# A two-layer encoder on one core: the MLP's down projections as seven block products in place of eight

## The reference, cut to what matters

```python
for i in range(2):
    h = h + mixer_i(rms_norm(h, norm_mix[i]))          # layer 0: conv + attention, layer 1: RWKV-7
    h = h + cross_attention(rms_norm(h, norm_xattn[i]), rms_norm(mem, norm_mem[i]), ...)
    h = h + squared_relu_mlp(rms_norm(h, norm_ffn[i]), ffn_w_up[i], ffn_w_down[i])
return rms_norm(h, norm_final)

def squared_relu_mlp(h, w_up, w_down):                 # (512, 1024), (1024, 4096), (4096, 1024)
    return jnp.square(jax.nn.relu(h @ w_up)) @ w_down
```

## Time and profile before

| | |
|---|---|
| device time, median of 3 | 1913.2 us (1911.54 to 1913.42) |
| span of the profiled execution, first to last instruction | 1909.6 us |
| TensorE busy | 97% of the span |
| VectorE, ScalarE, GpSimd busy | 55%, 39%, 9% |
| memory traffic | 189 MB, mean 99 GB/s |

### The profile page before, as it was taken

The page is one execution under the profiler, slowest core; times in us unless marked ns, Lnnn a source line. Parts: engine busy times, 40 slices in busy tenths (PEclk is TensorE's granted clock), DMA queues, the critical chain, the costliest instruction groups (busy, mean ns, idle before and its releaser), DMA issues.

```text
span 1909.6 us, 38661 instructions
## 1 busy us (share of the span) xinstructions
PE 1857.5 (97%) x17053; PEld 1527.4 (80%) x17053; DVE 1052.6 (55%) x1405; ACT 747.2 (39%) x999; POOL 168.8 (9%) x135
## 2 busy tenths in 40 slices
PE   6999999999999999999999999999999999999997
PEld 5898658778888888785779999998787788888886
DVE  4897655444432442447659888887654344324422
ACT  4434664334422332223544434343643343213322
POOL 1000002000000000210013111111020010000000
PEclk9999999999999999999999999999999999999999
DMA  6226223213332232453442112112362123332221
GB/s 215 89 71 233 78 100 133 66 45 93 106 111 88 89 111 88 137 159 127 154 147 62 51 50 53 49 31 70 126 217 70 44 89 102 97 110 89 88 88 44
DMA packets 165503, 189.41 MB, mean 99 GB/s; under 512 B 11801, under 2 KB 152646, under 8 KB 163674
## 3 DMA queue, kind: packets, MB, share of 16 engines
q1 hardware_dynamic: 162016, 174.44, 28.8%
q0 software_dynamic: 3088, 12.45, 1.7%
q10 hardware_dynamic: 234, 0.06, 0.0%
HBM read 161.22 MB, written 21.51 MB: 96 GB/s over the span
## 4 chain that ended last, share of the span: by engine, by line
PE 51%; DVE 3%; ACT 2%; issue 1%; DMA 1%; ACTq 0%; DVEq 0%
PE ps L357 11%; PE ps L358 10%; PE ps L359 10%; PE ps L2372 7%; PE ps L2338 2%; PE ps L2385 1%; PE ps L2326 1%; PE ps L1706 1%; PE ps L2349 1%; PE ps L1313 1%; PE ps L1746 1%; PE ps L2468 1%; ACT weights_split L326 1%; PE ps L2305 1%; PE ps L1294 1%
## 5 line engine op out<-in xcount | busy, mean ns | idle before, releaser
L344 DVE TENSOR_TENSOR weights_split<-w,weights_split 128x2048 fp32r<-128x2048 f32 x117 | 268.1, 2291 | 243.1 <-ACT weights_split L326 238.2
L326 ACT ACTIVATE weights_split<-w 128x2048 fp32r<-128x2048 f32 x118 | 225.9, 1914 | 285.7 <-PE ps L359 265.9
L357 PE MATMUL ps<-x_hn_hi,weights_split 128*128 128x512 f32 x640 | 252.7, 395 | 0.0
L359 PE MATMUL ps<-x_hn_hi,weights_split 128*128 128x512 f32 x640 | 249.2, 389 | 0.0
L358 PE MATMUL ps<-x_hn_lo,weights_split 128*128 128x512 f32 x640 | 249.0, 389 | 0.0
L357 PE MATMUL ps<-f_hidden_hi,weights_split 128*128 128x512 f32 x512 | 199.3, 389 | 0.0
L359 PE MATMUL ps<-f_hidden_hi,weights_split 128*128 128x512 f32 x512 | 199.2, 389 | 0.0
L358 PE MATMUL ps<-f_hidden_lo,weights_split 128*128 128x512 f32 x512 | 199.2, 389 | 0.0
L1565 DVE SCALAR_TENSOR_TENSOR f_relu<-ps,x_squares 128x512 f32<-128x512 f32 x64 | 44.1, 692 | 191.1 <-PE ps L359 172.5
L358 PEld LDWEIGHTS ps<-x_hn_lo,weights_split 128*128 128x128 f32 x640 | 120.2, 188 | 26.3 <-issue 1.4
L357 PEld LDWEIGHTS ps<-x_hn_hi,weights_split 128*128 128x128 f32 x640 | 120.1, 188 | 26.2 <-issue 1.4
(11 more groups left out here) (365 smaller groups left out, 3464.0 us busy)
## 6 DMA issues: line engine op xcount, KB each, us to landing
w<-in_ffn_w_up_dram SPq DMA_DIRECT2D x32, 1024.0 KB, 5.4
w<-in_ffn_w_down_dram SPq DMA_DIRECT2D x32, 1024.0 KB, 5.0
w<-in_xattn_w_kv_dram SPq DMA_DIRECT2D x15, 1024.0 KB, 5.4
w<-in_ab_w_in_dram SPq DMA_DIRECT2D x10, 1024.0 KB, 5.1
w<-in_xattn_w_q_dram SPq DMA_DIRECT2D x8, 1024.0 KB, 5.0
w<-in_xattn_w_o_dram SPq DMA_DIRECT2D x8, 1024.0 KB, 4.9
w<-in_ab_w_out_dram SPq DMA_DIRECT2D x4, 1024.0 KB, 5.5
w<-in_rwkv_w_r_dram SPq DMA_DIRECT2D x4, 1024.0 KB, 5.9
```

The costliest lines, as they stand in the source:

```text
L326: act.activation(hi, raw, ACT.Copy).then_inc(k.w_hi_ready, 1)
L344: eng.tensor_tensor(lo, raw, hi.bitcast(F32), ALU.subtract).then_inc(k.w_lo_ready, 1)
L357: pe.matmul(out, lhs[0], rhs[0], start=start, stop=False)
L359: return pe.matmul(out, lhs[1], rhs[0], start=False, stop=stop)
```

## The change

The MLP runs in four quarters of 1024 hidden channels. In each, the product of the hidden values (512 x 1024) with the down weights (1024 x 1024) is cut into halves of all three dimensions, and the eight products of blocks become seven products of sums of blocks, with four differences of weight blocks and four sums of hidden blocks. A product (P1 to P7) has the hidden values as the stationary operand and weights as the moving one, so results are token rows: two tiles of 128 tokens x 512 channels, 24 matmuls of 512 columns with 128 rows in the array. There are 7 units of weights in a quarter to be split, each used for 24 matmuls; before, a quarter's worth was 4 slots of 48. VectorE makes the four differences of raw weights (`combine`, 128x2048), GpSimd the sums of hidden blocks (three of 128x256) and their remainders (128x768) for each of the 4 hidden blocks of a quarter. Finished products are taken out of PSUM by VectorE into two sums of token rows (`take`, 14 of 128x512 a quarter). Five products share banks 4 to 7 one behind the other (`FORMER`), so P4, say, may begin when P7 is taken.

At the end of layer 0 the token rows are transposed back in 32 transposes and added to h, then squared and added up, all of it behind the last product. In layer 1, h is transposed to token rows during the first quarter (32 transposes, copied by ScalarE), and the output's norm is computed on token rows, rows 2 and 3 (tokens 256 to 511) ahead of the last product's end. A fourth raw buffer (`f_weights`) lies over the squares' buffers; its first load waits for the norm's factor.

```diff
@@ plan_weights, in layer_tail (one quarter: 4 slots of up weights, then 4 blocks of down weights) @@
-            for half in range(0, FF, FF // 2):
-                cols(f"up{l}", i["ffn_w_up"][l], half, half + FF // 2)
-                for c in range(0, D, SLOT):
-                    for r in range(half, half + FF // 2, D):
-                        cols(f"down{l}", i["ffn_w_down"][l], c, c + SLOT, r)
+            for r in range(0, FF, D):
+                cols(f"up{l}", i["ffn_w_up"][l], r, r + D)
+                rows = i["ffn_w_down"][l][r:r + D, :].rearrange("(j k p) c -> k p j c", k=2, p=P)
+                for b, n in ((0, 1), (1, 1), (0, 0), (1, 0)):
+                    self.slots.append((f"down{l}", [(None, None, rows[b, :, :, n * D // 2:(n + 1) * D // 2])]))
...
+                    x12, x22, x11, x21 = range(s - 3, s + 1)
+                    n = len(self.units)
+                    self.units += [(x11, 0), (x21, 0), (x11, sums + 1), (x11, sums + 3), (x22, 0), (x12, sums + 2),
+                                   (x21, sums + 4)]
@@ Split: the difference of two raw weight blocks, written over one of them @@
+    def combine(self, dve, i, a, b):
...
+        dve.tensor_tensor(flat(s), flat(sa), flat(sb), ALU.subtract).then_inc(k.w_sums, 1)
@@ stage_layer @@
+    PRODUCTS = (("P1", 0, 4, 0, 0, 0), ("P2", 3, None, 1, 0, 0), ("P5", 4, 6, 2, 1, 1), ("P6", 5, 4, 3, 0, 1),
+                ("P3", 6, 6, 4, 0, 1), ("P7", 1, 4, 5, 1, 1), ("P4", 2, 4, 6, 1, 0))
+    FORMER = {"P6": ("P1", 0), "P3": ("P5", 0), "P7": ("P6", 0), "P4": ("P7", 0), "P1": ("P4", 1), "P5": ("P3", 1)}
...
@@ TensorE @@
+            def down(q):
+                for x, (name, part, bank, u, half, right) in enumerate(PRODUCTS):
+                    ws.wait(pe, WF + NS * q + 4 + u)
...
+                        mm = mm3(pe, outs[m], [h[:, j, part, m * P:(m + 1) * P] for h in hid],
+                                 ws.wide_pair(WF + NS * q + 4 + u, j), j == 0 and name in ("P1", "P2", "P5"), j == 3,
+                                 bank is not None)
...
+                    if last and q == 0:
+                        for c in (2 * a, 2 * a + 1):
+                            k.take(pe, turned[c])
+                            for t in range(4):
+                                m = pe.transpose(k.bank(turned[c])[:, t * P:(t + 1) * P],
+                                                 k.h[:, c, t * P:(t + 1) * P], k.ident)
...
+            if not last:
+                for n, c in enumerate(TURN):
+                    k.take(pe, turned[n])
...
+                squares[2].sum(pe)
@@ ScalarE @@
+            for q in range(4):
                 for a in range(4):
...
+                    for m in range(3):
+                        b = PARTS[m]
+                        if m == 1:
+                            ws.round(act, WF + NS * q + a + 2)
+                        if m < 2:
+                            k.wait_freed(act, up[q][2 * a + m])
+                            r = tm[:, 3 * m:3 * m + 2, :]
+                            act.activation(r, r, ACT.Square).then_inc(s_hsq, 1)
...
+                        else:
+                            act.wait_ge(s_hsum, 2 * y + 1)
+                        act.activation(hid[0][:, a, b.start - 1:b.stop - 1, :], tm[:, b, :], ACT.Copy).then_inc(s_hhi, 1)
...
+                for x in range(7):
+                    ws.round(act, WF + NS * q + 4 + x + 2)
@@ VectorE @@
+            for q in range(4):
...
                 for a in range(4):
...
+                    relu(q, a, 0)
...
+                    dve.tensor_tensor(tm[:, 2, :], tm[:, 1, :], tm[:, 0, :], ALU.subtract).then_inc(s_hd, 1)
+                    remainder(q, a, 0)
+                    relu(q, a, 1)
+                    ws.rest(dve, W + a + 2)
+                    remainder(q, a, 1)
+                    if a == 2:
+                        ws.combine(dve, U + 2, U + 5, U)
+                    elif a == 3:
+                        ws.combine(dve, U + 5, U + 4, U + 5)
+                for x in range(7):
...
+                    late = x in (0, 1, 3)
+                    if not late:
+                        take(q, x)
+                    ws.rest(dve, U + x + 2)
+                    if x == 0:
+                        ws.combine(dve, U + 3, U + 4, U + 2)
+                    elif x == 2:
+                        ws.combine(dve, U + 6, U + 1, U + 3)
+                    if late:
+                        take(q, x)
+                    if last and q == 3 and x == 4:
...
+                        for t in (2, 3):
+                            root(t, t + 3)
+                            scaled(t, 0)
+                            scaled(t, 1)
...
+                for n, c in enumerate(TURN):
+                    k.wait_full(dve, turned[n])
+                    dve.tensor_tensor(k.h[:, c, :], k.bank(turned[n]), k.h[:, c, :], ALU.add) \
@@ GpSimd @@
+            for y in range(y0, y0 + 16):
+                pool.wait_ge(s_hsq, 2 * y + 2)
...
+                k.pool.link(pool, pool.tensor_tensor(tm[:, 5, :], tm[:, 0, :], tm[:, 3, :], ALU.add))
+                k.pool.link(pool, pool.tensor_tensor(tm[:, 6, :], tm[:, 5, :], tm[:, 1, :], ALU.subtract))
+                pool.tensor_tensor(tm[:, 7, :], tm[:, 4, :], tm[:, 6, :], ALU.subtract).then_inc(s_hsum, 1)
+                pool.wait_ge(s_hhi, 3 * y + 3)
+                pool.tensor_tensor(hid[1][:, y % 4, 4:7, :], tm[:, 5:8, :], hid[0][:, y % 4, 4:7, :].bitcast(F32),
+                                   ALU.subtract).then_inc(s_hsum, 1)
```

More of the change, by code:

```diff
@@ L262, in split_room, with slot_plan @@
         self.w_lo = [room[:, 3], room[:, 1]]
-    def slot_plan(self, jobs, split=True):
+    def slot_plan(self, jobs, split=True, slots=None):
         s0 = self.at
@@ L284, in w_wait @@
     def w_wait(self, pe, s):
-        need = sum(16 * len(self.slots[t][1]) for t in range(s % NW, s + 1, NW))
-        pe.wait_ge(self.w_in[s % NW], need)
+        b = self.buffers[s]
+        need = sum(16 * len(self.slots[t][1]) for t in range(s + 1) if self.buffers[t] == b)
+        pe.wait_ge(self.w_in[b], need)
 class Split:
@@ L296, in __init__ @@
         self.k, self.base = k, k.splits
-        assert k.to_split[self.base] == s0, "slots are split in order"
+        assert k.units[self.base][0] == s0, "slots are split in order"
         k.splits += len(ends)
@@ L469, in sum @@
         pe.matmul(bank, self.k.ones, self.sq[:, 1, :], start=False, stop=True).then_inc(self.s_ss, 1)
-    def columns(self, pe):
-        bank = self.k.ps[:, 7, :]
-        for src, ready in ((self.acc, (self.s_acc, self.acc0 + C - 2)), (self.sq[:, 1, :], (self.s_sq, self.sq0 + C))):
-            pe.wait_ge(*ready)
-            for t in range(4):
-                m = pe.matmul(bank[:, t:t + 1], src[:, t * P:(t + 1) * P], self.k.ones[:, 0:1],
-                              start=src is self.acc and t == 0, stop=src is not self.acc, skip_group_check=True)
-        m.then_inc(self.s_ss, 1)
     def stats(self):
@@ L1168, in stage_layer @@
     nc = k.nc
-    H = FC // 2
     KB = 1024
@@ L1361, in _ @@
+            for q in range(4):
+                for a in range(4):
+                    i = WF + NS * q + a
+                    if q == a == 0:
+                        mm3_first(pe, k, up[0][0], ws, b_pair.both, lambda c: hf.wait(pe, c), WF)
+                        squares[1].sum(pe)
+                    else:
                         ws.wait(pe, i)
                         for m in range(2):
-                            n = down[half] + 2 * a + m
-                            if d == 0:
-                                k.take(pe, n)
@@ new lines, in _ @@
+                down(q)
+            if not last:
+                for n, c in enumerate(TURN):
+                    k.take(pe, turned[n])
+                    if c >= 4:
+                        pe.wait_ge(k.s_ptaken, kept("P7", 3, 1) + 1)
+                    else:
+                        pe.wait_ge(k.s_ptaken, kept("P4", 3, 1) + 1)
+                        for m in range(2):
+                            k.wait_freed(pe, side[3] + m)
+                    for t in range(4):
+                        m = pe.transpose(k.bank(turned[n])[:, t * P:(t + 1) * P],
+                                         sums[c // 4][:, t, c % 4 * P:(c % 4 + 1) * P], k.ident)
+                    m.then_inc(k.done(turned[n]), 1)
@@ new lines, in _ @@
+            if last:
+                for t in range(2):
+                    dve.wait_ge(s_osq, o0 + 7 + t)
+                    dve.tensor_tensor(sums[1][:, t, :], sums[1][:, t, :], gain[:, T:D], ALU.mult)
+                for t in range(2):
+                    take(3, 6, (t,))
+                    mean(t, 9 + 2 * t)
+                    root(t, 10 + 2 * t)
+                    scaled(t, 0)
+            if not last:
+                for n, c in enumerate(TURN):
+                    k.wait_full(dve, turned[n])
+                    dve.tensor_tensor(k.h[:, c, :], k.bank(turned[n]), k.h[:, c, :], ALU.add) \
```

(1 more changed line is left out.)

414 lines of the change are left out of this document (241 added, 173 removed).

## The result

The changed kernel takes 1950.1 us (median of 4, 1947.99 to 1953.99), the kernel before 1912.5 (1911.54 to 1913.42): ratio 1.0199, 95% interval 1.0184 to 1.0213. The direction was forecast, the size was not: +9.9 forecast, +37.6 measured, above the range.

The account below looks back on a forecast made before the run. TensorE, full in the MLP, was taken as the bound. Span 1909.6 - 43.5 + 38.4 + 13.0 + 2.0 + 0 = 1919.5; the median 3.6 above gives 1923 us. Range 1894 to 1938; forecast's own range 1915 to 1930.

Parts of the forecast that it names:

- matmuls removed: MLP down products: 1536 matmuls become 1344, each removed one worth 0.2267 us, -43.5 us.
- eight seams: Between up and down products: TensorE stalls for split weights at P5 and P6, +38.4 us in all (34.8 to 42.4).
- end of layer 0: After layer 0's last product: chain of takes, squares and GpSimd adds +11.2, clock 1.8; +13.0 us (+9 to +14).
- transposes, first quarter of layer 1: All 32 transposes now in these up products, 16 of them formerly in the loop, 0.12 us each: +2.0 us.
- tail with P4's hold: Layer 1's end: scaling delays P7's take, so P4 waits 5.9 us, plus 1.8 for clock; net 0 (-6 to +2).
- Together 4.8 a seam: Each seam: P5 stalls 3.7 us and P6 1.06 as VectorE and GpSimd take turns; 4.35 to 5.3 by GpSimd's rate.
- the rival with 0.15: TensorE's clock falls at every seam, 1.8 us at each of eight, giving 1937 us; chance 0.15.
- the prediction's own last sign of being wrong: The forecast is wrong if the clock level falls at the seams; no size given.
- It decides if the sums are ready before 6.4: Test at P5 for the rival of no hold that matters: 0.5 us a seam, 1889 us, chance 0.13.
- the sums get through: Rival at the seams: GpSimd's third sum precedes the weight difference, P5 stalls 1.7, 2.8 a seam, 1907 us; chance 0.15.
- the takes (hidden under 5.44 us of products): VectorE's takes of finished down products, costed at nothing, since each product lasts 5.44 us.
- Late loads: Rival: three weight loads share the engines, each up part starts 3 us late, 1940 us; chance 0.05.

Follow-up runs that it names:

- second profile: The changed kernel run again unedited, to get another profile: 1946.2 us, ratio 1.0186 to the kernel before.
- with both down: Changed kernel with the second weight difference moved to the second down product and P5's weights rounded ahead of the last block's sums: 1927.2 us.
- the worse order: Changed kernel, P5's weights rounded ahead of the sums, second weight difference at the third down product, third behind P6's take: 1940.5 us.
- the first profile: Profile of the changed kernel's first measurement (median 1950.1 us), taken from its longest execution, 1953.99 us.
- the good order: Changed kernel, P5's weights rounded ahead of sums; second and third differences at second and third down products, P2's take after P6, only P6's first tile early: 1907.0 us.
- the filled gap: Changed kernel with 14 extra matmuls, results overwritten, run in place of TensorE's wait for P5's weights at seven of eight seams: 1942.8 us.

## Why the prediction was off, point by point

Forecast and second profile, in us of span:

| term | forecast | measured |
|---|---|---|
| matmuls removed | -43.5 | -43.5 (pace 0.2267 kept) |
| eight seams | +38.4 | +60.2 |
| end of layer 0 | +13.0 | +12.4 |
| transposes, first quarter of layer 1 | +2.0 | +6.2 |
| tail with P4's hold | 0 | +0.7 |
| untouched parts | 0 | +0.1 |
| sum | +9.9 | +36.1 |

**The mis-sized step is "Together 4.8 a seam".** Its mechanism held: P5's wait 3.76 for 3.7, P6's 1.03 for 1.06 once the clock is kept up, GpSimd's sum of 256 elements 0.74 alone for 0.74, of 768 1.84 for 1.8. The rule of the Trainium skill (SBUF — State Buffer, "Who interferes with whom"), a lock for the whole instruction, agrees: 2.67 under a difference, 0.74 without. What a seam cost was 7.2, and three things were missing (in the seam shown 0.6 for P2, 0.2 that P5's wait with its restart is above 3.7, 2.6 for the clock, less the 1.06 of P6). *P2's wait*: my ledger had its weights just in time (5.4 of 5.44), they were 0.45 late (0.6 with the restart), since ScalarE began the rounding 0.5 later than I had it. *The clock*: it fell at all eight seams, as the rival with 0.15 said, and as the prediction's own last sign of being wrong has it. In the seam shown 6.72 - 18 x 0.2267 = 2.6 us are lost to it, of which P6's wait, with its restart, pays 1.2 back. The rival had 1.8 for the fall *and* P6's wait; the two can't both be had. *The first quarter of layer 0*: its hidden chain starts late, at the norm's factor, and recovers only 0.45 us a block (10.43 against 10.88), so P1 and P2 waited 2.48 and 1.74; that makes 3 to 4 us, since I had taken the quarters to be alike.

**"It decides if the sums are ready before 6.4"** and **"the sums get through"** put it on one race at P5. The runs show four more places where the same stall can stand: with P5's wait down to 0.9, P6 took 2.4; with both down, P3 and P7 took 1.8 together; in the worse order P4 took 1.95. What I costed at nothing, "the takes (hidden under 5.44 us of products)", is hidden only in a suitable order.

**The end of layer 0** was right in the sum (12.4 of 13.0) and in the wait (7.9 of about 7). The clock did fall there (granted 0.50 from 813.60 to 823.66), but was up again when the next stage began (0.99 to 837), so it slowed only the two matmuls of the sum: 4.26 us from the first to the next stage where the prediction had 2.96, 1.3 for the clock, not 1.8.

**Transposes**: eight took 0.8 us, 0.10 each. (The 6.2: layer 1's first quarter of up products took 53.1 us, 9.6 over its 192 matmuls; 1.8 were there before, and 1.6 stood elsewhere in the MLP.) Missing was their effect on the banks: with two of four in use, the third hidden chunk waits for the first relu (2.72). Behind that wait the level fell in the second profile and not in the first, where the same up products took 51.7 us: 1.4 of the 6.2 are this fall.

**The tail**: 8.3 for hold and clock against 7.7 forecast, 6.4 behind the last product as forecast.

**Late loads**: no. A load of the next up weights took 8.1 us from issue to landing in the first profile (three together, and 9.1 for the one in the fourth buffer) where the prediction had 5.4, and no up product waited for one.

What stays open: how much of each fall of the level depends on where in time it meets the wait. The seams of one execution differ, 6.4 to 7.5 above their matmuls at equal waits, and the eight executions of the unedited kernel lie between 1943.6 and 1954.0 us.

## What to carry to other kernels

A stall taken from one instruction of a full in-order pipeline goes to the next one that stood behind the same queue; cost an order for the whole period, each consumer with its due time, before calling a chain fixed. Here four orders made by moving one or a few instructions at single waits stayed 13 to 32 us over the kernel before, and one order of the same instructions, found that way, went below it.

A wait of TensorE costs its length plus the slow stretch that can stand behind it, minus what later waits the slow stretch hides. Read the granted clock by stage with the number of matmuls in it, not the busy share; a few filler matmuls in one run separate the two.

Where an engine starts a stage late for a norm's factor, the first period is not like the others: take its chain's period against the slot and see whether the lag is made up.

## What the runs showed of the hardware that I had not expected

- Behind a wait of 3.76 us, with 24 matmuls before it at 1.00, the level of 1.2 GHz came at every seam. Behind a pair of waits of 1.0 and 1.95 us with one product between them it came in six of seven seams of the worse order. Waits of 0.45 and 0.61, in six seams of the good order, brought none. In between the same wait did both: 1.8 us before P5 at three of eight seams (the difference moved alone), 2.4 before P6 at four of eight (the rounding moved alone), 2.48 in layer 0's first quarter in five of thirteen profiles, 2.72 for the relu in eight of twelve. What decides between them stays open. The Trainium skill (TensorE: Matmul & The Clock Gate, Part 1) has the low level as the default that activity lifts; the filled gap agrees with it.
- A wait costs more than the idle time shown: between the starts of the matmuls on both sides of P5's wait lie 4.14 us, 3.91 more than the pace, at 3.76 of idle time. The 0.15 between is what a matmul's record (0.39) is longer than the pace (0.23).
